# A hybrid attention, retention and expert trunk on one core: probabilities in two steps, the gates made ahead of the first tiles' low parts, rows and 1 / rms made by GpSimd

## The chip, the core and the metric

The kernel runs on one core of a Trainium2 chip. The time is device microseconds of one execution. PE is TensorE, DVE is VectorE, ACT is ScalarE, POOL is GpSimd and SP is SyncE, which here only issues DMAs.

## What is computed

Two layers over 256 rows of 1024 values. Each layer: RMS norm, one input projection of 2304 columns, of which some feed a windowed softmax attention with sinks (8 heads) and the others a gated retention (4 heads); both outputs are concatenated, projected back and added. Then RMS norm and a SwiGLU: dense in layer 0, and in layer 1 eight experts of which each row takes the best two. A last RMS norm ends it. The parts that the change touches are the softmax and the routing:

```
    m = jnp.maximum(jnp.max(s, axis=-1, keepdims=True), sink)
    p = jnp.exp(s - m)
    p = p / (jnp.sum(p, axis=-1, keepdims=True) + jnp.exp(sink - m))
    o = jnp.einsum('bgrcqk,bckgd->bcqgrd', p.astype(v.dtype), vw)
...
    logits = (h @ router_w).astype(f32)
    top_val, top_idx = lax.top_k(logits, TOP_K)
    top_w = jax.nn.softmax(top_val, axis=-1)
    gates = jnp.sum(jax.nn.one_hot(top_idx, N_EXPERTS, dtype=f32) * top_w[..., None], axis=-2)
    y = jnp.zeros_like(h)
    for e in range(N_EXPERTS):
        y = y + gates[..., e:e + 1].astype(h.dtype) * swiglu(h, w_gate[e], w_up[e], w_down[e])
```

## The kernel before

**Weights in pieces.** All weights stream through a ring of 11 slots (`raw`), a unit of 128 x 2048 values each, filled by SP. A unit is worked in two pieces of 128 x 1024. For each piece ACT makes the high part, a rounded copy (`w_hi`, 6 slots, L397 in the front, L417 in the experts), DVE the low part, what is left (`w_lo`, 3 slots, L406 and L424), and PE multiplies in `piece` (L1264): first all products with the high part, activations' high and low tiles (`aT_hi`, `aT_lo`) in turn, then, behind a wait on `lo_vec`, those of the high tiles with the low part. Its last product raises `piece_used`, which frees the slots: DVE may make the low part of piece p once piece p - 3 is used. SP refills a unit's slot when its second low part is made (`lo_vec`).

**The order of work is written out by hand.** On every engine a loop over the pieces s of a mixing stage (26 in a layer: 18 of the input projection, 8 of the output projection) has, at fixed s, the other work in front of the high or low part due there. In DVE's loop (L936) step s makes the low part of piece s + 3 at its end. At s = 7 the scores get bias and maxima, at s = 9 DVE adds up the denominators, takes reciprocals and makes the probabilities in eight operations of 128 x 256 (L979 to L983, chunks 1 and 3 first), each raising `prob_ready`. PE transposes them at s = 12 (`PROB_TURN`, L1365), behind piece 12, when all eight are there. POOL turns the retention's queries and keys (`rope`, L531) at its steps 7 and 9, on two-operand operations between tiles of SBUF.

**The start of the experts.** Behind layer 1's mixing stage PE makes the router's logits; DVE picks the best two of each row (`hot1`, `hot2`), their sum `mask` (L1093), the difference of the two logits (L1095), then 1 / rms (`norm_factor(3)`, L876 to L880) and the scaled gap (L1097) for ACT's exponential `e2` (L775). PE ranks the rows per expert from `mask` (L1494), filling the time with products nobody reads (`keep_busy`). DVE makes `posx` and from it `pick` (L1109), the one-hot matrices with which PE gathers the first pair of experts' rows (`gather`, L1499), high and low parts of the rows (`xg_hi` by ACT, `xg_lo` by DVE, L1151). ACT copies what is gathered into four tiles of `aT_hi` (L782), and `gather_low` (L1111) makes the low tiles on DVE. Tiles 0 and 1 must be there for PE's piece 0, tile 2 for piece 4, tile 3 for piece 6 (L1568).

DVE's order there is: `pick`, the pass count `passes_i` (L1147), `xg_lo`, `gather_low` of tiles 0 and 1 (L1152), the low part of piece 0 (L1154), the slots of the second pass (L1155), then behind ACT's `e2` the gates (L1158 to L1163), the row numbers (L1166, L1167), 1 / rms for every expert (L1168) and a copy (L1169) whose end raises `info_ready`; then it loads the pass count into a register (L1172), enters the loop over passes (L1204) and makes the low parts of pieces 1 and 2 (L1176), and so on. `info` (128 x 2 x 8 x 3: 1 / rms, gate, row) is read by PE in `gather_info` (L1515), behind piece 1 of each even expert, which gives every slot its three numbers; DVE's `slot_info` (L1116) turns them into scales and row addresses. The operations of the gates hang together by semaphores:

```
    def __call__(self, ins):
        self.n += 1
        ins.then_inc(self.sem, 1)
        self.eng.wait_ge(self.sem, self.n)
```

`link(...)` waits for its operation's end, `link.also(...)` only counts it.

POOL's queue (L528) holds at this point: behind `xg_made` the load of the last norm's gain (L582), then the wait for the pass count, its register, and the scatter of each expert's output, which waits for that expert.

Of the kernel before, what the change touches and what calls it, by code (L numbers as in the profile page):

```python
# [11 lines left out]
ALU = mybir.AluOpType  # L12
# [3 lines left out]
P = 128  # L16
SEQ, D_MODEL, DEPTH = 256, 1024, 2
# [63 lines left out]
RET_SCORE = {15: (0, 1), 16: (2, 3)}  # L81
EXP_CHUNKS = {7: (0, 1), 8: (2, 3)}
# [8 lines left out]
C_ALL = C_ROW + TT  # L91
# [8 lines left out]
def constants():  # L100
# [16 lines left out]
    for t in range(TT):  # L117
# [4 lines left out]
        c[:, C_ROW + t] = t * P + n - NO_ROW  # L122
    return c
# [31 lines left out]
def trunk(nc, x, ln_mix, w_in, w_out, rel_bias_table, sinks, ln_ffn, ffn_w_gate, ffn_w_up, ffn_w_down,  # L155
          router_w, exp_w_gate, exp_w_up, exp_w_down, ln_final, consts, buckets, zeros, out):
    with ExitStack() as ctx:
# [49 lines left out]
        def at(name, offset, shape, dt=F32):  # L207

            return nc.alloc_sbuf_tensor_at(name, shape, dt, offset=base_of + offset)
# [36 lines left out]
        passes_f = at("passes_f", 18048, [P, 1])  # L246
        logits_T = at("logits_T", 16384, [N_EXPERTS, SEQ])
# [95 lines left out]
        down_half = sem("down_half")  # L343
        info_ready, row_made, oe_made, scattered = sem("info_ready"), sem("row_made"), sem("oe_made"), sem("scattered")
# [183 lines left out]
        def _(pool):  # L528
# [53 lines left out]
            pool.dma_start(gain_last, ln_final.partition_broadcast(P)).then_inc(gain_landed, 16)  # L582
            pool.wait_ge(route_ready, 1)
# [286 lines left out]
        def _(dve):  # L870
# [46 lines left out]
            for layer in range(DEPTH):  # L917
# [18 lines left out]
                for s in range(MIX_PIECES):  # L936
# [36 lines left out]
                    if s == 9:  # L973
# [5 lines left out]
                        for c0, dst0, src0 in ((1, 0, 0), (1, 64, 64), (0, 0, 64), (0, 64, 0)):  # L979
# [172 lines left out]
            for b in range(2):  # L1152
                gather_low(0, b)
            low_part_e(dve, 0, 0)  # L1154
# [8 lines left out]
            link.also(dve.tensor_tensor(info[:, :, :, 1], gates, tmp, ALU.add))  # L1163
            for t in range(TT):
                step = link if t == TT - 1 else link.also
                step(dve.tensor_scalar(rest[:, t, :], mask[:, t, :], cst[:, C_ROW + t:C_ROW + t + 1], None, ALU.mult))  # L1166
            link.also(dve.scalar_tensor_tensor(out=info[:, :, :, 2], in0=hot2, scalar=float(SEQ), in1=rest, op0=ALU.mult, op1=ALU.add))  # L1167
            link(dve.tensor_copy(info[:, :, :, 0], wide(rstd[:, 2, :])))  # L1168
            dve.tensor_copy(table_first[:], info[:, 0, 0, 0:1]).then_inc(info_ready, 1)  # L1169
# [33 lines left out]

            with dve.Fori(0, n_pass) as r:  # L1204
                with dve.If(r > 0):
                    dve.wait_ge(pick_turned, r)
                    dve.tensor_scalar(info[:, :, :, 2], info[:, :, :, 2], float(ROWS), None, ALU.add).then_inc(info_ready, 1)
# [26 lines left out]
        def _(pe):  # L1234
# [280 lines left out]
            def gather_info(r, e):  # L1515

                pe.wait_ge(info_ready, r + 1)
# [134 lines left out]
```

## Time and profile before

| | us |
|---|---|
| Runs, median of three (lowest, highest) | 1179.99 (1178.19, 1183.70) |
| Profiled execution | 1179.01 |
| Its span | 1177.20 |
| Share of the span that PE, DVE, ACT and POOL are busy | 98%, 81%, 70%, 4% |
| Mean granted clock of PE | 0.996 |

How to read the rows: a time is in us from the span's start. A timeline's row has start, duration, engine, line of the kernel, operation, what it writes and reads with shapes, and the number of operations it merges; a bracket at its end says how long the engine stood idle before it and what ended that. Operations on an engine overlap at their ends, so that starts lie closer together than the durations say. The layer-0 mixing stage runs from about 30 to 104 us, layer 0's dense stage to 292, the layer-1 mixing stage to 385, the router and the start of the experts to about 410, and the experts to the end.

### The profile page before, as it was taken

What the parts mean: (1) busy time and instruction counts of PE and PEld (TensorE: products, weight loads), DVE (VectorE), ACT (ScalarE), POOL (GpSimd) and SP (SyncE); (2) the same over time, 40 slices, a digit from 0 to 9 for tenths busy, and PEclk for the clock granted to TensorE, in tenths of its full rate; (3) what the DMA queues carried; (4) which work ended last, traced back from release to release, by engine and by line L of the source; (5) the groups of instructions that cost most, each with busy time, mean ns of one, the idle gap of its engine ahead of it and who ended that gap; (6) DMA issues with size and microseconds to landing.
All of it is one profiled execution on the core that took longest, in us unless ns stands there. A gap on an engine that the chain in (4) does not pass through costs nothing.

```text
span 1177.2 us, 18157 instructions
## 1 busy us (share of the span) xinstructions
PE 1156.5 (98%) x5954; PEld 971.7 (83%) x5954; DVE 958.5 (81%) x1071; ACT 828.8 (70%) x1003; POOL 43.3 (4%) x57
## 2 busy tenths in 40 slices
PE   9999999999999899999999999999999999999996
PEld 8997888888998688888888888888888888888785
DVE  5867555545676799999899989989999989998996
ACT  6655544433653678788788888878888878888785
POOL 0400000000130000000000000000000000000000
PEclk9999999999999999999999999999999999999999
DMA  9965678556444199999999999999999999999960
GB/s 283 371 190 166 194 248 280 184 179 200 159 154 148 53 348 369 389 385 369 368 337 376 358 398 375 357 345 365 370 394 373 373 339 381 365 369 393 375 271 36
DMA packets 144295, 352.78 MB, mean 300 GB/s; under 512 B 6766, under 2 KB 65342, under 8 KB 144144
## 3 DMA queue, kind: packets, MB, share of 16 engines
q1 hardware_dynamic: 141808, 341.81, 80.3%
q0 software_dynamic: 2032, 9.23, 2.2%
q8 instruction: 50, 0.82, 0.3%
q10 hardware_dynamic: 368, 0.62, 0.2%
q14 instruction: 37, 0.30, 0.1%
HBM read 348.35 MB, written 9.31 MB: 304 GB/s over the span
## 4 chain that ended last, share of the span: by engine, by line
PE 87%; DVE 5%; DMA 3%; ACT 2%; issue 2%; SPq 0%; DVEq 0%; ACTq 0%; POOLq 0%
PE psum L1239 84%; PE psum L1236 3%; DMA raw<-in_w_in 1%; DMA scratch<-oe,row_e 1%; DVE prob L982 1%; DMA back<-scratch 1%; DVE w_lo L424 1%; DVE w_lo L406 1%; DVE smax L966 0%; ACT w_hi L397 0%; DVE score L962 0%; DMA skew<-bias_rows 0%; DVE proj L1015 0%; DVE nmax L967 0%; ACT L723 0%
## 5 line engine op out<-in xcount | busy, mean ns | idle before, releaser
L424 DVE TENSOR_TENSOR w_lo<-raw,w_hi 128x1024 fp32r<-128x1024 f32 x528 | 631.4, 1223 | 47.9 <-PE psum L1239 15.0
L417 ACT ACTIVATE w_hi<-raw 128x1024 fp32r<-128x1024 f32 x528 | 550.6, 1061 | 104.7 <-PE psum L1239 103.6
L1239 PE MATMUL psum<-w_hi,aT_hi 128*128 128x512 f32 (+1 forms) x1232 | 446.1, 371 | 2.6 <-ACT aT_hi L782 1.6
L1239 PE MATMUL psum<-w_hi,aT_lo 128*128 128x512 f32 (+1 forms) x1232 | 439.1, 365 | 0.0
L1239 PE MATMUL psum<-w_lo,aT_hi 128*128 128x512 f32 (+1 forms) x1232 | 323.3, 366 | 5.4 <-DVE w_lo L424 4.6
L1239 PEld LDWEIGHTS psum<-w_hi,aT_hi 128*128 128x128 f32 x1232 | 232.8, 189 | 40.4 <-issue 3.4
L1239 PEld LDWEIGHTS psum<-w_hi,aT_lo 128*128 128x128 f32 x1232 | 232.8, 189 | 35.3
L1239 PEld LDWEIGHTS psum<-w_lo,aT_hi 128*128 128x128 f32 x1232 | 214.4, 189 | 45.0 <-DVE w_lo L424 6.3
L406 DVE TENSOR_TENSOR w_lo<-raw,w_hi 128x1024 fp32r<-128x1024 f32 x118 | 144.8, 1234 | 47.6 <-PE psum L1239 45.8
L397 ACT ACTIVATE w_hi<-raw 128x1024 fp32r<-128x1024 f32 x118 | 124.6, 1060 | 81.0 <-PE psum L1239 74.1
L1239 PE MATMUL psum<-w_hi,heT_hi 128*128 128x512 f32 x352 | 137.8, 391 | 0.0
L1239 PE MATMUL psum<-w_hi,heT_lo 128*128 128x512 f32 x352 | 137.1, 389 | 0.0
L1239 PE MATMUL psum<-w_lo,heT_hi 128*128 128x512 f32 x352 | 108.5, 389 | 0.0
L1239 PEld LDWEIGHTS psum<-w_lo,heT_hi 128*128 128x128 f32 x352 | 66.1, 188 | 13.8
L1239 PEld LDWEIGHTS psum<-w_hi,heT_lo 128*128 128x128 f32 x352 | 66.1, 188 | 13.5
L1239 PEld LDWEIGHTS psum<-w_hi,heT_hi 128*128 128x128 f32 x352 | 66.1, 188 | 13.4
L829 ACT ACTIVATE heT_hi<-psum 128x512 fp32r<-128x512 f32 (+1 forms) x48 | 27.1, 564 | 26.3 <-PE psum L1236 26.3
L1193 DVE TENSOR_TENSOR heT_lo<-psum,heT_hi 128x512 fp32r<-128x512 f32 (+1 forms) x48 | 31.1, 647 | 5.2 <-ACT heT_hi L829 4.8
L824 ACT ACTIVATE hid_e<-psum,info_e 128x512 f32<-128x512 f32 (+1 forms) x48 | 29.5, 651 | 7.3 <-PE psum L1239 7.3
L1239 PE MATMUL psum<-w_hi,hdT_hi 128*128 128x512 f32 x88 | 34.3, 390 | 0.0
L1239 PE MATMUL psum<-w_hi,hdT_lo 128*128 128x512 f32 x88 | 34.3, 389 | 0.0
L1186 DVE SCALAR_TENSOR_TENSOR hid_e<-psum,info_e,hid_e 128x512 f32<-128x512 f32 (+1 forms) x48 | 32.4, 704 | 2.1 <-PE psum L1239 2.1
(194 smaller groups left out, 598.7 us busy)
## 6 DMA issues: line engine op xcount, KB each, us to landing
raw<-in_exp_w_down SPq DMA_DIRECT2D x88, 1024.0 KB, 7.0
raw<-in_exp_w_gate SPq DMA_DIRECT2D x80, 1024.0 KB, 7.0
raw<-in_exp_w_up SPq DMA_DIRECT2D x80, 1024.0 KB, 7.4
raw<-in_w_in SPq DMA_DIRECT2D x17, 1024.0 KB, 5.4
raw<-in_ffn_w_gate SPq DMA_DIRECT2D x22, 512.0 KB, 4.1
raw<-in_ffn_w_up SPq DMA_DIRECT2D x22, 512.0 KB, 5.2
raw<-in_ffn_w_down SPq DMA_DIRECT2D x11, 1024.0 KB, 5.0
raw<-in_w_out SPq DMA_DIRECT2D x8, 1024.0 KB, 8.6
```

The costliest lines, as they stand in the source:

```text
L397: nc.scalar.activation(high_slot(p), raw_piece((p // 2) % RING, p % 2), ACT.Copy).then_inc(hi_made, 1)
L406: eng.tensor_tensor(low_slot(p), raw_piece((p // 2) % RING, p % 2), high_slot(p).bitcast(F32), ALU.subtract).then_inc(lo_vec, 1)
L417: nc.scalar.activation(w_hi[:, q % HIGHS, :], raw_piece(slot, q % 2), ACT.Copy).then_inc(hi_made, 1)
L424: eng.tensor_tensor(w_lo[:, q % LOWS, :], raw_piece(e_slot[q // 2], q % 2), w_hi[:, q % HIGHS, :].bitcast(F32), ALU.subtract).then_inc(lo_ ...
L824: nc.scalar.activation(hid_e[:, c % 2, 0:E_CHUNKS[c][1]], gate_chunk(c), ACT.Silu, scale=info_e[:, e // 2 % 2, j, 0:1]).then_inc(e_gate, 1)
L829: nc.scalar.activation(heT_hi[:, col // P:(col + width) // P, :], psum[:, 4 + c % 2, 0:width].rearrange("p (k t) -> p k t", t=P), ACT.Copy ...
L982: dve.tensor_tensor(prob[:, c, :, dst0:dst0 + 64], score[:, c, :, src0:src0 + 64], r, ALU.mult).then_inc(prob_ready, 1)
L1186: dve.scalar_tensor_tensor(out=part, in0=up_chunk(c), scalar=info_e[:, e // 2 % 2, j, 0:1], in1=part, op0=ALU.mult, op1=ALU.mult).then_inc ...
L1193: dve.tensor_tensor(heT_lo[:, cols, :], psum[:, 4 + c % 2, 0:width].rearrange("p (k t) -> p k t", t=P), heT_hi[:, cols, :].bitcast(F32), A ...
L1236: return pe.matmul(dst, src, ident, is_transpose=True, start=True, stop=True, skip_group_check=True)
L1239: return pe.matmul(dst, a, b, start=start, stop=stop, skip_group_check=True)
```

## The change

Attention's probabilities: four of the eight operations stay at s = 9, the other four move to s = 10, behind the low part of piece 12. At the start of the experts, DVE makes the slots of the second pass and the gates in front of the first `gather_low`, loads its register there too, and leaves the last operation of the gates to raise `info_ready`. The row numbers and the 1 / rms column go to POOL as four operations of 128 x 16 (a product of mask and row, a product of `hot2` and the constant 256, their sum, and ones by 1 / rms), with a semaphore `info_rows` that `gather_info` on PE waits for. The copy L1169 is gone. The constants get one column more.

```diff
+PROB_STEP = {9: ((1, 0, 0), (1, 64, 64)), 10: ((0, 0, 64), (0, 64, 0))}
...
+        row_parts = at("row_parts", 18240, [P, 2, TT, N_EXPERTS])
...
             pool.wait_ge(xg_made, TT)
             pool.dma_start(gain_last, ln_final.partition_broadcast(P)).then_inc(gain_landed, 16)
+            pool.wait_ge(mask_made, 1)
+            mask = mask3[:, 0:TT * N_EXPERTS].rearrange("p (t e) -> p t e", t=TT)
+            row = cst[:, C_ROW:C_ROW + TT].unsqueeze(2).to_broadcast([P, TT, N_EXPERTS])
+            step = cst[:, C_STEP:C_STEP + 1].unsqueeze(2).to_broadcast([P, TT, N_EXPERTS])
+            one = cst[:, C_ONE:C_ONE + TT * N_EXPERTS].rearrange("p (t e) -> p t e", t=TT)
+            pool.tensor_tensor(row_parts[:, 0, :, :], mask, row, ALU.mult).then_inc(row_links, 1)
+            pool.tensor_tensor(row_parts[:, 1, :, :], rt[1][:], step, ALU.mult).then_inc(row_links, 1)
+            pool.wait_ge(row_links, 2)
+            pool.tensor_tensor(info[:, :, :, 2], row_parts[:, 0, :, :], row_parts[:, 1, :, :], ALU.add).then_inc(info_rows, 1)
+            pool.wait_ge(rstd_made, 4)
+            pool.tensor_tensor(info[:, :, :, 0], one, rstd[:, 2, :].unsqueeze(2).to_broadcast([P, TT, N_EXPERTS]), ALU.mult).then_inc(info_rows, 1)
             pool.wait_ge(route_ready, 1)
...
-                        for c0, dst0, src0 in ((1, 0, 0), (1, 64, 64), (0, 0, 64), (0, 64, 0)):
+                    if s in PROB_STEP:
+                        for c0, dst0, src0 in PROB_STEP[s]:
...
-            for b in range(2):
-                gather_low(0, b)
-            low_part_e(dve, 0, 0)
             link.also(dve.tensor_scalar(posx[:, :, 8:16], posx[:, :, 0:8], -float(P), None, ALU.add))
...
-            link.also(dve.tensor_tensor(info[:, :, :, 1], gates, tmp, ALU.add))
-            for t in range(TT):
-                step = link if t == TT - 1 else link.also
-                step(dve.tensor_scalar(rest[:, t, :], mask[:, t, :], cst[:, C_ROW + t:C_ROW + t + 1], None, ALU.mult))
-            link.also(dve.scalar_tensor_tensor(out=info[:, :, :, 2], in0=hot2, scalar=float(SEQ), in1=rest, op0=ALU.mult, op1=ALU.add))
-            link(dve.tensor_copy(info[:, :, :, 0], wide(rstd[:, 2, :])))
-            dve.tensor_copy(table_first[:], info[:, 0, 0, 0:1]).then_inc(info_ready, 1)
+            dve.tensor_tensor(info[:, :, :, 1], gates, tmp, ALU.add).then_inc(info_ready, 1)
 
             dve.wait_ge(route_ready, 1)
             n_pass = dve.value_load(passes_i[0:1, 0:1], min_val=1, max_val=2)
...
+            for b in range(2):
+                gather_low(0, b)
+            low_part_e(dve, 0, 0)
             with dve.Fori(0, n_pass) as r:
                 with dve.If(r > 0):
                     dve.wait_ge(pick_turned, r)
+                    dve.wait_ge(info_rows, 2)
...
                 pe.wait_ge(info_ready, r + 1)
+                pe.wait_ge(info_rows, 2)
```

## Rows read from the trace of the kernel before

**Rows 1.** The page: busy time of the engines, and the last chain by engine.
```profile
PE 1156.5 (98%) x5954; PEld 971.7 (83%) x5954; DVE 958.5 (81%) x1071; ACT 828.8 (70%) x1003; POOL 43.3 (4%) x57
...
PE 87%; DVE 5%; DMA 3%; ACT 2%; issue 2%; SPq 0%; DVEq 0%; ACTq 0%; POOLq 0%
```

**Rows 2.** The waits of PE: who released it, us in total, times, longest.
```profile
PE psum L1239 <- DVE w_lo L424: 4.6, 3, 2.7
PE psum L1239 <- ACT aT_hi L782: 1.6, 1, 1.6
...
PE psum L1239 <- DVE w_lo L406: 0.7, 2, 0.4
```

**Rows 3.** The timeline of PE, layer 0 and 1: start us, us, engine, line, operation.
```profile
55.79 1.22 PE L1239 MATMUL psum<-w_lo,aT_hi 128*128 128x256 f32 x8 [0.37 <-DVE w_lo L406]
...
336.89 1.22 PE L1239 MATMUL psum<-w_lo,aT_hi 128*128 128x256 f32 x8 [0.35 <-DVE w_lo L406]
```

**Rows 4.** The timeline of DVE, layer 1: the probabilities and the rows around them.
```profile
325.09 0.41 DVE L967 SCALAR_TENSOR_TENSOR nmax<-smax,nsinkc 128x4 f32<-128x4 f32 x1
...
326.87 0.16 DVE L967 SCALAR_TENSOR_TENSOR nmax<-smax,nsinkc 128x4 f32<-128x4 f32 x1
...
330.31 5.06 DVE L982 TENSOR_TENSOR prob<-score,rden 128x256 f32<-128x256 f32 x8
335.29 3.00 DVE L406 TENSOR_TENSOR w_lo<-raw,w_hi 128x1024 fp32r<-128x1024 f32 x2
```

**Rows 5.** The timeline of PE at the start of the experts.
```profile
402.67 0.49 PE L1239 MATMUL psum<-w_hi,aT_hi 128*128 128x512 f32 x1 [1.56 <-ACT aT_hi L782]
...
404.85 0.40 PE L1239 MATMUL psum<-w_hi,aT_lo 128*128 128x512 f32 x1
407.94 0.73 PE L1239 MATMUL psum<-w_lo,aT_hi 128*128 128x512 f32 x2 [2.69 <-DVE w_lo L424]
...
409.32 0.49 PE L1239 MATMUL psum<-w_hi,aT_hi 128*128 128x512 f32 x1
...
416.50 0.39 PE L1239 MATMUL psum<-w_hi,aT_hi 128*128 128x512 f32 x1
...
417.86 0.39 PE L1239 MATMUL psum<-w_hi,aT_hi 128*128 128x512 f32 x1
```

**Rows 6.** The timeline of DVE at the start of the experts.
```profile
394.60 0.15 DVE L1095 TENSOR_TENSOR rc<-rc,rc 128x2 f32<-128x2 f32 x1
...
396.02 0.88 DVE L1109 TENSOR_SCALAR pick<-cst,posx 128x128 fp32r<-128x128 f32 x4
...
401.06 1.29 DVE L1113 TENSOR_TENSOR aT_lo<-psum,aT_hi 128x512 fp32r<-128x512 f32 x2 [1.63 <-ACT aT_hi L782]
402.27 1.22 DVE L424 TENSOR_TENSOR w_lo<-raw,w_hi 128x1024 fp32r<-128x1024 f32 x1
...
403.48 0.16 DVE L1158 TENSOR_SCALAR rc<-rc 128x2 f32<-128x2 f32 x1
...
404.37 0.18 DVE L1163 TENSOR_TENSOR info<-rt,rt 128x16 f32<-128x16 f32 x1
...
405.15 0.15 DVE L1169 COPY table_first<-info 128x1 f32<-128x1 f32 x1
406.67 3.50 DVE L424 TENSOR_TENSOR w_lo<-raw,w_hi 128x1024 fp32r<-128x1024 f32 x3 [1.35 <-ACT w_hi L417]
```

**Rows 7.** The register load in DVE's queue, by source line (ns min/median/max).
```profile
L1172 DVEq TENSOR_LOAD <-passes_i x1: 546/546/546, 405.2 to 405.2; - x1
```

**Rows 8.** Stretches of 0.5 us: busy time of the engines, PEclk (granted clock), DMA.
```profile
410.50:411.00 0.50, 0.50 (x3) 0.40 (x2) 0.50 (x2) 0.00 (x0) 0.00 (x0) 0.50 1.07 434
...
413.00:413.50 0.50, 0.50 (x3) 0.40 (x2) 0.50 (x1) 0.00 (x0) 0.00 (x0) 0.50 1.01 418
```

**Rows 9.** The timeline of POOL, layer 1: rope.
```profile
324.15 0.52 POOL L548 TENSOR_TENSOR rope_tmp<-proj,cst 128x128 f32<-128x128 f32 x1
324.75 0.73 POOL L551 TENSOR_TENSOR proj<-proj,rope_tmp 128x256 f32<-128x256 f32 x1
```

More of the change, by code:

```diff
@@ L90 @@
 C_ROW = C_RANK + TT * N_EXPERTS
-C_ALL = C_ROW + TT
+C_STEP = C_ROW + TT
+C_ALL = C_STEP + 1
 CHOSEN = 1000.0
@@ L122, in constants @@
         c[:, C_ROW + t] = t * P + n - NO_ROW
+    c[:, C_STEP] = SEQ
     return c
@@ L343, in trunk @@
         down_half = sem("down_half")
+        info_rows, row_links = sem("info_rows"), sem("row_links")
         info_ready, row_made, oe_made, scattered = sem("info_ready"), sem("row_made"), sem("oe_made"), sem("scattered")
```

## The prediction

> **What bounds the kernel.** I read the busy shares and the last chain first: PE is busy for 98% of the span and makes up 87% of the chain [rows 1]. So a saving on another engine counts only where PE waits for it. The waits of PE are the second view, and they are short: DVE's low parts L424 hold it for 4.6 us in three waits, the longest 2.7, and the low parts L406 for 0.7 us in two [rows 2]. The timelines give the places. The two waits for L406 are one in each layer, 0.37 and 0.35 us, both in front of the low products of a piece of the input projection [rows 3], and in front of both DVE works through eight tiles of probabilities, 5.06 us from 330.31 in layer 1, with the low part next at 335.29 [rows 4]. The wait of 2.69 us is at the first expert: PE starts piece 0 at 402.67, is through with the high products of piece 1 at 405.25 (404.85 and 0.40) and gets that piece's low part at 407.94 [rows 5]. What DVE did meanwhile is in [rows 6]: the low part of piece 0 from 402.27, then the gates, rows and copies from 403.4 to 405.30, a load of a register of 0.55 us from 405.2 [rows 7], the loop's entry, and the low part of piece 1 only at 406.67. Behind this the granted clock is 0.50, that is 1.2 GHz, from 410.50 to 413.50 [rows 8]; PE had been idle for 1.56 and 2.69 us in the eight microseconds before.
>
> **The sum, against the profiled execution's own 1179.01 us** (span 1177.20, 1.81 around it). The median of the three runs is 0.98 above it, and I carry that over at the end.
>
> 1. Probabilities in two steps. DVE does the same eight operations, but the low part of piece 12 now comes after four. By 5.06 / 8 the four end at 330.31 + 2.53 = 332.84, and the low part, 1.5 us beside POOL's rope (3.00 for two), at about 334.3 instead of 336.84. PE asks for it at 336.89 - 0.35 = 336.54, so both waits go: 0.35 + 0.37 = **0.72 us off**. What is late next: the other four end at 334.3 + 2.5 = 336.8, and PE wants them when it has done piece 12's low products, 1.22 behind 336.54, less a little for the last one's tail: 337.6. The next low part ends at 338.3 as before. Margin 0.8 us, so nothing new is waited for. Bounds: 0 if something else holds PE at the same place, 0.72 if not.
>
> 2. Gates first. DVE is idle for 1.63 us before the first `gather_low`, at 399.43 to 401.06 [rows 6]. L1155 and the gates now stand there. L1158 to the start of L1163 took 404.37 - 403.48 = 0.89, so L1163 starts at about 400.3. The register load is issued behind it: in the trace it starts at 405.2, before L1169 has ended, so the queue runs ahead of the engine [rows 6, 7]. From L1169's start at 405.15 the load and its two register operations take until about 406.0, 0.9 us in all; from 400.3 and with the waits of the queue that is 401.35. The first low tile thus starts 0.3 us late, its pair takes 1.29, and PE starts piece 0 at 403.0 instead of 402.67. Hence the low part of piece 0 ends at 403.8 and, with nothing between, that of piece 1 at 403.8 + 3.50 / 3 = 405.0. The loop's entry is now passed by the queue while the 1.22 us low part runs, so I cost it at nothing; without that cover low part 1 would end 0.6 us later and PE wait 0.3 us. PE issues a product each 1.36 / 6 = 0.23 us, so it could have gone on to piece 1's low products at 404.85 + 0.23 = 405.08, and 0.33 later, at 405.41, it can now. The low part is there at 405.0, so they start at 405.41 instead of 407.94: **2.53 us off**, the 0.33 us of lateness being in it.
>
> 3. Rows, 1 / rms and the copy leave DVE: five instructions, 404.46 to 405.30. They are inside the wait of part 2, since everything between the two low parts is; no second saving. Who needs them is PE's gather of the slot data behind piece 1, at about 405.8 now. POOL can begin at the mask, which stands in front of L1095 at 394.60 [rows 6]; even four operations of 0.73 us end at 397.6 or, behind 1 / rms, not much later. Eight microseconds of cover: costed at nothing. POOL's queue holds only the load of the last gain ahead, and nobody waits for what is behind.
>
> 4. The clock. From piece 2's start at 409.32 to piece 7's at 417.86 are 8.54 us for five pieces; at full clock one takes 1.36 (416.50 to 417.86), so 6.80. The half clock costs 1.74 us [rows 5, 8]. With the longer of the two idle stretches gone I expect the clock to hold: **1.74 us off**; bounds 0 and 1.74. DVE keeps up with that: from 405.0 on it has two more pieces by 407.3, a gathered tile (0.65) by 408.0, then a piece, a tile and a piece by 411.0, and PE wants these at 407.7, 409.5 and 411.8.
>
> 5. POOL beside DVE. This goes against the change. In layer 1 DVE's L967 reads two tiles of SBUF and takes 0.16 us with POOL at rest, but 0.41 when it starts at 325.09, and then ends at 325.50, just when POOL's L551 ends (324.75 + 0.73) [rows 4, 9]. So DVE's small two-operand operations wait for the end of POOL's. In the new place POOL's four operations fall on L1095, L877, L878, L880 and L1097, five such ones on the chain to `pick` at 396.02, for which PE waits. POOL's 16 elements aren't in the trace. The nearest rows are 0.52 for 128 and 0.73 for 256 elements [rows 9]; drawn on to 16 that is 0.33. The longest delay is all of POOL's work, 4 x 0.52 = 2.1 us, the least nothing. DVE also has one-operand steps between, and POOL waits for its own links, so I take a third of 4 x 0.33: **0.4 us on**. The Trainium skill, "SBUF — State Buffer", "Who interferes with whom", says that a VectorE operation with two SBUF inputs contends with a GpSimd one that reads SBUF, and whoever comes second is blocked for the whole of the other; the trace agrees by the 0.41. By it alone the price would be up to POOL's whole time.
>
> Sum: 1179.01 - 0.72 - 2.53 - 1.74 + 0.40 = 1174.42; with the 0.98 of the median, **1175.4 us**, 0.4% less. Later stages are bound by PE, and SP's loads start with the low parts, earlier by as much, so the gain goes through to the end.
>
> **Rivals.**
> - The clock falls all the same, since 1.56 us of idle before piece 0 stay and grow by 0.3, and PE is idle for longer before the gather. For it: one fall is all that the trace has here, so which of the two stretches made it can't be told. Against: the fall came behind the longer. 1175.4 + 1.74 = 1177.1.
> - The port. POOL blocks DVE for all of its time, 2.1 instead of 0.4: 1175.4 + 1.7 = 1177.1. For it the ends that meet at 325.50; against, POOL's operations here are 16 elements wide. The page of the Trainium skill named above is the rule behind this one.
> - The split gains nothing, because PE then stands before the transposes of the probabilities: 1175.4 + 0.7 = 1176.1. Its margin of 0.8 us speaks against.
> - The change doesn't do what it says: DVE waits for ACT's exponential before the gates, and that comes late. Then `gather_low` moves behind it; ACT had it well before 399.4 though, as DVE is idle there for the tiles alone. A microsecond late gives 1176.4.
> - Slower: the mark chain of PE is held by POOL for 2.1 us, PE stands idle before the gather, and the clock falls there, so that the gather (32 products, some 4 us from `pick` to the tiles at 401) and the first pieces run at 1.2 GHz. Price 2.1 + 3 for the gather, with the old fall kept (1.74) and another as long (1.74). Against 1175.0, the sum without part 5 and with the median's 0.98, that is 1183.6. It decides from 5.0 us on, where all gains are eaten.
> - More than I see: the three runs lie between 1178.19 and 1183.70, and if the falls of the clock behind this idle stretch make that scatter, the median gains more: some 1173.
>
> **Chances.** My forecast 0.58, the clock 0.14, the port 0.08, the split 0.07, the late exponential 0.03, slower 0.03, more 0.07. The range: at the bottom all gains and no port cost, 1175.0, less the 1.8 us by which the lowest run lies below the median, 1173.2, so 1172.9 with the last case touched; at the top the clock and half of the port's extra together, 1175.4 + 1.74 + 0.85 = 1178.0, so 1178.2. What a measurement of this kernel can tell from no change is about 0.5%, 5.9 us. My own case gains 4.6, so faster by more than that takes the last case or a favourable scatter in mine: 0.18. Slower by as much needs more than the worst case: 0.01. Within: 0.81.
>
> **What would show it.** Right: no wait of PE for L406 in either layer; PE's low products of piece 1 follow its high ones with no idle; first low tile at about 0.3 us behind ACT's; clock 1.00 from 396 to 420; L1095 to `pick` 0.2 to 0.6 us longer than the 1.42 us of before. Wrong: a clock of 0.50 anywhere behind the gather; a new wait of PE for POOL's rows, or for `prob`; DVE idle between the low parts of pieces 0 and 1; low parts from piece 3 on that PE waits for.

## The result, and the profile after

| | before | after |
|---|---|---|
| Median of six runs, us (lowest, highest) | 1180.95 (1178.19, 1183.70) | 1174.15 (1172.70, 1174.66) |
| Profiled execution, us | 1179.01 | 1173.32 |
| Its span, us | 1177.2 | 1171.5 |
| Mean granted clock | 0.996 | 0.998 |

The ratio is 0.9941, with a 95% interval of 0.9925 to 0.9956: the kernel is 0.6% faster, by 4.4 to 7.5 thousandths. The line numbers below are those of the kernel after: `piece` multiplies at L1252, DVE's low parts are L412 and L430, `gather_low` is L1131, the last of the gates L1178.

The waits of PE (total us, times, longest) answer to [rows 2]:

```profile
PE psum L1252 <- ACT w_hi L403: 1.7, 1, 1.7
PE psum L1252 <- DVE aT_lo L1131: 1.7, 1, 1.7
PE psum L1252 <- DVE w_lo L430: 1.6, 2, 1.3
```

The 2.69 us behind L430 and both waits for the low parts of the front (0.35 and 0.37) are gone. What is left at L430 are two waits in the last experts, 1.31 us (1.61 before) and 0.34 us as before. The wait before piece 0 (1.68 us) is as long as it was, and DVE's low tile ends it, where ACT's high tile did. The 1.7 us for ACT's L403 is at the kernel's start and belongs to no part of the change: the kernel before has it too in its two later profiles (e11 and e12 below).

The probabilities in layer 1, on DVE (to [rows 4]) and the piece behind them on PE (to [rows 3]):

```profile
329.86 1.98 DVE L1000 TENSOR_TENSOR prob<-score,rden 128x256 f32<-128x256 f32 x4
331.76 1.55 DVE L412 TENSOR_TENSOR w_lo<-raw,w_hi 128x1024 fp32r<-128x1024 f32 x1
333.23 3.17 DVE L1000 TENSOR_TENSOR prob<-score,rden 128x256 f32<-128x256 f32 x4
```

```profile
335.93 1.12 PE L1252 MATMUL psum<-w_lo,aT_hi 128*128 128x256 f32 x8
336.89 1.91 PE L1249 MATMUL psum<-cst,prob 128*128 128x128 f32 x16
```

The low part of piece 12 now ends at 333.31; PE asks for it at 335.93, goes on without a pause, and turns the probabilities from 336.89, half a microsecond after the last of them (333.23 + 3.17 = 336.40).

The start of the experts, DVE (to [rows 6]), then PE (to [rows 5]):

```profile
393.54 0.15 DVE L1113 TENSOR_TENSOR rc<-rc,rc 128x2 f32<-128x2 f32 x1
...
395.01 0.87 DVE L1127 TENSOR_SCALAR pick<-cst,posx 128x128 fp32r<-128x128 f32 x4
...
399.30 0.18 DVE L1178 TENSOR_TENSOR info<-rt,rt 128x16 f32<-128x16 f32 x1
400.24 1.29 DVE L1131 TENSOR_TENSOR aT_lo<-psum,aT_hi 128x512 fp32r<-128x512 f32 x2 [0.76 <-ACT aT_hi L799]
401.45 4.62 DVE L430 TENSOR_TENSOR w_lo<-raw,w_hi 128x1024 fp32r<-128x1024 f32 x4
```

```profile
401.78 0.49 PE L1252 MATMUL psum<-w_hi,aT_hi 128*128 128x512 f32 x1 [1.68 <-DVE aT_lo L1131]
...
403.97 0.40 PE L1252 MATMUL psum<-w_hi,aT_lo 128*128 128x512 f32 x1
404.20 0.62 PE L1252 MATMUL psum<-w_lo,aT_hi 128*128 128x512 f32 x2
...
405.47 0.49 PE L1252 MATMUL psum<-w_hi,aT_hi 128*128 128x512 f32 x1
...
412.41 0.39 PE L1252 MATMUL psum<-w_hi,aT_hi 128*128 128x512 f32 x1
```

Four low parts follow each other from 401.45, where 3.2 us lay between the first and the second. Piece 1's low products start 0.23 us behind its last high one. From piece 2 (405.47) to piece 7 (412.41) are 6.94 us instead of 8.54. The clock, in stretches with the columns of [rows 8] (the third number from the right is the granted clock; 1.00 is 2.4 GHz):

```profile
402.00:406.00 4.00, 4.00 (x22) 3.32 (x22) 4.00 (x5) 4.00 (x5) 0.00 (x0) 1.00 0.21 32
406.00:410.00 4.00, 4.00 (x19) 3.27 (x18) 3.97 (x9) 2.44 (x4) 0.00 (x0) 1.00 1.00 396
```

This profile is at half clock only at its very end, from 1166.9 us, where PE has no products left. Every profile here ends so, the one of before from 1171.5, and the mean clock of the table counts this stretch too.

POOL's four new operations, in its timeline:

```profile
393.71 0.21 POOL L594 TENSOR_TENSOR row_parts<-mask,cst 128x16 f32<-128x16 f32 x1 [2.94 <-DVE mask L1111]
393.89 0.21 POOL L595 TENSOR_TENSOR row_parts<-rt,cst 128x16 f32<-128x16 f32 x1
394.18 0.23 POOL L597 TENSOR_TENSOR info<-row_parts 128x16 f32<-128x16 f32 x1
394.70 0.22 POOL L599 TENSOR_TENSOR info<-cst,rstd 128x16 f32<-128x16 f32 x1 [0.30 <-DVE rstd L897]
```

They take 0.21 to 0.23 us and are over at 394.92, almost ten microseconds before PE asks for the rows. DVE's chain from L1113 to `pick` is 395.01 - 393.54 = 1.47 us beside them; it was 396.02 - 394.60 = 1.42.

So the profiles alone, by the same product of PE in both: at piece 12's low part of layer 1 the new kernel is 0.96 us ahead (336.89, 335.93), at the experts' first product 0.89 (402.67, 401.78), at piece 1's low part 3.74 (407.94, 404.20), at piece 7 5.45 (417.86, 412.41), at the end 5.7. The forecast's sum was 4.59. Of the 0.96 us at the first of these, 0.72 are the two waits, the rest lies further up and belongs to no part of the change; of the last step, from 5.45 to 5.7, 0.3 us are the shorter wait at the last experts. The medians are further apart, by 6.8 us: the kernel before has a median 1.94 us above its profiled execution, the kernel after one 0.83 above. The experiments had to explain that gap as well.

### The profile page after: what moved, and what is told of

Read it like the earlier page. It is cut to its first block, busy times and chain, and to the rows that moved or that the text cites. A ratio compares the mean times of both kernels' runs of the same rounds, so it can differ in the third digit from the quotient of the medians.

```text
span 1171.5 us, 18160 instructions
## 1 busy us (share of the span) xinstructions
PE 1152.5 (98%) x5954; PEld 969.0 (83%) x5954; DVE 957.4 (82%) x1066; ACT 828.5 (71%) x1003; POOL 44.6 (4%) x61
## 4 chain that ended last, share of the span: by engine, by line
PE 92%; DVE 2%; DMA 2%; ACT 2%; issue 1%; DVEq 0%; SPq 0%; ACTq 0%; POOLq 0%
PE psum L1252 89%; PE psum L1249 3%; DMA scratch<-oe,row_e 1%; DMA raw<-in_w_in 1%; DMA back<-scratch 1%; DVE w_lo L430 0%; ACT w_hi L403 0%; DVE proj L1033 0%; ACT L740 0%; DVE w_lo L412 0%; ACT proj L740 0%; ACT aT_hi L726 0%; DVE x_sb L926 0%; ACT o_sq L734 0%; DVE proj L1040 0%
## 5 line engine op out<-in xcount | busy, mean ns | idle before, releaser
L430 DVE TENSOR_TENSOR w_lo<-raw,w_hi 128x1024 fp32r<-128x1024 f32 x528 | 630.8, 1221 | 45.3 <-PE psum L1252 13.8
L1252 PE MATMUL psum<-w_hi,aT_hi 128*128 128x512 f32 (+1 forms) x1232 | 445.6, 371 | 4.0 <-ACT w_hi L403 1.7
L1252 PE MATMUL psum<-w_hi,aT_lo 128*128 128x512 f32 (+1 forms) x1232 | 438.6, 365 | 0.0
L1252 PE MATMUL psum<-w_lo,aT_hi 128*128 128x512 f32 (+1 forms) x1232 | 322.2, 365 | 1.6 <-DVE w_lo L430 1.6
L1252 PEld LDWEIGHTS psum<-w_hi,aT_hi 128*128 128x128 f32 x1232 | 232.3, 189 | 41.6 <-issue 3.5
L1252 PEld LDWEIGHTS psum<-w_hi,aT_lo 128*128 128x128 f32 x1232 | 232.5, 189 | 35.1
L1252 PEld LDWEIGHTS psum<-w_lo,aT_hi 128*128 128x128 f32 x1232 | 214.0, 189 | 40.5 <-DVE w_lo L430 3.1
L412 DVE TENSOR_TENSOR w_lo<-raw,w_hi 128x1024 fp32r<-128x1024 f32 x118 | 144.9, 1234 | 47.7 <-PE psum L1252 45.9
L403 ACT ACTIVATE w_hi<-raw 128x1024 fp32r<-128x1024 f32 x118 | 124.5, 1059 | 81.4 <-PE psum L1252 74.2
L1252 PE MATMUL psum<-w_hi,heT_hi 128*128 128x512 f32 x352 | 137.8, 391 | 0.0
L1252 PE MATMUL psum<-w_hi,heT_lo 128*128 128x512 f32 x352 | 137.1, 389 | 0.0
L1252 PE MATMUL psum<-w_lo,heT_hi 128*128 128x512 f32 x352 | 108.5, 389 | 0.0
L1252 PEld LDWEIGHTS psum<-w_lo,heT_hi 128*128 128x128 f32 x352 | 66.1, 188 | 13.8
L1252 PEld LDWEIGHTS psum<-w_hi,heT_lo 128*128 128x128 f32 x352 | 66.1, 188 | 13.5
L1252 PEld LDWEIGHTS psum<-w_hi,heT_hi 128*128 128x128 f32 x352 | 66.1, 188 | 13.4
L611 POOL DMA_INDIRECT scratch<-oe,row_e x7 | 9.3, 1332 | 663.8 <-ACT oe L810 560.6
L1252 PE MATMUL psum<-w_hi,hdT_hi 128*128 128x512 f32 x88 | 34.3, 390 | 0.0
L1252 PE MATMUL psum<-w_hi,hdT_lo 128*128 128x512 f32 x88 | 34.3, 389 | 0.0
```

Source lines behind the costliest of these rows:

```text
L403: nc.scalar.activation(high_slot(p), raw_piece((p // 2) % RING, p % 2), ACT.Copy).then_inc(hi_made, 1)
L412: eng.tensor_tensor(low_slot(p), raw_piece((p // 2) % RING, p % 2), high_slot(p).bitcast(F32), ALU.subtract).then_inc(lo_vec, 1)
L430: eng.tensor_tensor(w_lo[:, q % LOWS, :], raw_piece(e_slot[q // 2], q % 2), w_hi[:, q % HIGHS, :].bitcast(F32), ALU.subtract).then_inc(lo_ ...
L611: pool.indirect_dma_start(scratch, bass.IndirectOffsetOnAxis(ap=row_e[:, v % 2, j:j + 1], axis=0), oe[:], None, bounds_check=2 * ROWS - 1, ...
L1252: return pe.matmul(dst, a, b, start=start, stop=stop, skip_group_check=True)
```

## The experiments

Two theories stood at the beginning. By the first (A), the three savings add up as forecast, and the half clock follows PE's idle of 2.69 us. By the second (B), the clock falls for the idle before piece 0, or for any, and its recovery has nothing to do with the moved gates. There is one profile of each kernel, and three of the kernel before. Savings "by the ratio" are the ratio to the kernel before, run beside it, times its 1180 us; an interval in brackets is the 95% interval of the ratio.

### The split alone, and all but the split

```diff
 e1_split: the kernel before, and
+PROB_STEP = {9: ((1, 0, 0), (1, 64, 64)), 10: ((0, 0, 64), (0, 64, 0))}
...
-                        for c0, dst0, src0 in ((1, 0, 0), (1, 64, 64), (0, 0, 64), (0, 64, 0)):
+                    if s in PROB_STEP:
+                        for c0, dst0, src0 in PROB_STEP[s]:
 e2_no_split: the kernel after, and
-PROB_STEP = {9: ((1, 0, 0), (1, 64, 64)), 10: ((0, 0, 64), (0, 64, 0))}
+PROB_STEP = {9: ((1, 0, 0), (1, 64, 64), (0, 0, 64), (0, 64, 0))}
```

> The kernel before with the probabilities in two steps alone. By my sum both waits of PE for the low part of piece 12 go and nothing else moves: 0.7 us off (0.72), idle 2.69 us and the half clock at the first expert as before. By the rival that PE then stands before the transposes: 0, and a wait of PE for prob shows. A third, that the split also moves the start of the experts against the clock's fall, would give 0.7 and up to 1.7 more.

> The changed kernel with all eight probabilities in one step again. By my sum it keeps all but 0.7 to 0.9 us of the gain: some 5 us off the kernel before by the spans, idle in front of piece 1's low products gone, clock at 1.00. If the split had part in keeping the clock up, the half clock is back: 3.3 us off.

The split alone: 1178.78 us median, ratio 0.9989 (0.9977 to 1.0001), 1.3 us by the ratio. All but the split: 1175.29, ratio 0.9960 (0.9948 to 0.9973), 4.7 us by the ratio, where the whole change had 0.9941. The interval of the split reaches from 2.7 us to just beyond nothing, so the runs alone don't show it; that of the rest reaches from 3.2 to 6.1 us. In the traces the wait for the low part of piece 12 is absent in the one (PE waits for L426 three times, all at the experts) and back with 0.7 us in two in the other. The half clock at the first expert is still there with the split alone, and its profile shows something new in the windows:

```profile
407.00:408.00 1.00, 0.75 (x2) 0.65 (x3) 1.00 (x2) 0.00 (x0) 0.00 (x0) 0.50 0.00 0
...
412.00:413.00 1.00, 1.00 (x4) 0.71 (x4) 0.15 (x1) 0.22 (x1) 0.00 (x0) 0.50 1.01 381
...
414.00:415.00 1.00, 1.00 (x6) 0.83 (x5) 0.68 (x5) 0.37 (x1) 0.00 (x0) 1.00 0.30 119
```

The clock is at half from 406.8 to 413.6, for 6.8 us and not for 3.4, though PE's wait is the same (2.76 us, from 404.5 to 407.25). It falls within that wait, 2.3 us after its start; in the profile of before it fell 2.4 us after the wait's end (410.36, 407.94).

### The move without POOL

```diff
 e3_move_only: the kernel before, without the copy L1169 (the copy of 1 / rms raises info_ready), and
-            for b in range(2):
-                gather_low(0, b)
-            low_part_e(dve, 0, 0)
...
+            for b in range(2):
+                gather_low(0, b)
+            low_part_e(dve, 0, 0)
             with dve.Fori(0, n_pass) as r:
```

> The kernel before, with the first two low tiles and the low part of piece 0 moved behind gates and rows, all made by DVE, nothing on POOL (the copy L1169 is left out). DVE then comes to the first low tile some 0.75 us later than in the changed kernel, 0.95 us behind ACT's high tile, so PE stands idle for 2.4 instead of 1.7 us before piece 0 and then never for 2 us. Theory A (the clock falls for the idle in front of piece 1's low products): clock stays 1.00, 4.0 us off before. Theory B (any idle of over 2 us there): clock 0.50 for 3.4 us, 2.4 us off.

1176.86 us, ratio 0.9974 (0.9963 to 0.9985), 3.1 us, between the 4.0 of theory A and the 2.4 of theory B. The timeline of PE and the windows:

```profile
403.75 0.49 PE L1238 MATMUL psum<-w_hi,aT_hi 128*128 128x512 f32 x1 [2.37 <-ACT w_hi L417]
...
407.64 0.71 PE L1238 MATMUL psum<-w_lo,aT_hi 128*128 128x512 f32 x2
```

```profile
404.00:405.00 1.00, 1.00 (x4) 0.76 (x4) 1.00 (x2) 1.00 (x2) 0.00 (x0) 0.70 0.00 0
...
406.00:407.00 1.00, 1.00 (x4) 0.80 (x3) 1.00 (x2) 0.83 (x1) 0.00 (x0) 0.50 0.17 20
...
408.00:409.00 1.00, 1.00 (x11) 0.95 (x9) 1.00 (x3) 0.61 (x1) 0.00 (x0) 1.00 1.00 401
```

Now there is no wait in front of piece 1's low products, PE is idle for 2.37 us before piece 0, and the clock is at half from 404.4 to 407.8. Theory A in its narrow form is wrong: it isn't that one place. The idle before piece 0 can bring the fall as well when it is longer than the 1.49 to 1.68 us that it lasts in the kernels before and after. It need not: two of the twelve executions had a mean clock of 0.997 and 0.998, like the kernel after, and took 1174.99 and 1174.66 us. That makes POOL's part worth something that I had costed at nothing: with rows and 1 / rms on DVE, the first low tile comes later (at 402.22, 0.9 us behind ACT's tile, where the kernel after is 0.2 behind), and the clock goes with it. Run side by side, the means of this kernel and of e2, which differ in POOL's part alone, are 1.7 us apart.

### POOL without the move

```diff
 e4_pool_only: the kernel after, the probabilities in one step, and
+            for b in range(2):
+                gather_low(0, b)
+            low_part_e(dve, 0, 0)
             link.also(dve.tensor_scalar(posx[:, :, 8:16], posx[:, :, 0:8], -float(P), None, ALU.add))
...
-            for b in range(2):
-                gather_low(0, b)
-            low_part_e(dve, 0, 0)
             with dve.Fori(0, n_pass) as r:
```

> Rows and 1 / rms on POOL and the copy gone, but the two low tiles and the low part of piece 0 in front of the gates as before, no split. DVE's work between the two low parts is shorter by 0.8 us, so PE's idle is 1.9 instead of 2.69. Theory A with the fall bound to the length of this idle: if 1.9 us is short enough, clock stays at 1.00 and 0.8 + 1.7 = 2.5 us off; if not, 0.8 us off. POOL's price on the chain to pick shows too: 0.05 us as in the changed kernel.

1179.34 us, ratio 0.9993 (0.9982 to 1.0003): no difference that these runs can tell, 0.8 us by the ratio. PE's wait is shorter by 0.7 us, as expected, and the clock falls:

```profile
407.24 1.00 PE L1252 MATMUL psum<-w_lo,aT_hi 128*128 128x512 f32 x2 [1.98 <-DVE w_lo L430]
```

```profile
408.00:409.00 1.00, 1.00 (x7) 0.96 (x5) 1.00 (x2) 0.72 (x1) 0.00 (x0) 0.50 0.73 86
```

Of this profile 6.8 us (from 407.5) are at half clock. So 1.98 us of idle, 1.49 before piece 0 ahead of it, were still too much in this execution; shortening the wait without ending it brought about its own length, and that within the error.

### The idle filled, with DVE no faster

In both kernels PE makes products in unused banks that nobody reads, 11 in the long idle or 6 in the short one.

```diff
 e5_fill_long: the kernel before, and in piece(), between its high and its low products (between is 11 for piece 1 of the first expert, else 0)
+                for again in range(between):
+                    mm(bank(6 + again % 2), w_hi[:, 1, 0:P], w_hi[:, 1, 0:512], True, True)
 e6_fill_short: the kernel before, and
             gather(4)
+            pe.wait_ge(hi_made, FRONT_PIECES + 1)
+            fill(6)
```

> The kernel before, and PE makes 11 products that nobody reads (128x512, 0.23 us each, 2.5 us) between the high and the low products of the first expert's piece 1, in the idle of 2.69 us. DVE's low part comes no earlier. Theory A (that idle makes the clock fall): clock stays at 1.00 and the 1.6 to 1.7 us of the half clock alone are saved. Theory B (the 1.56 us before piece 0 make it fall, or it falls at any rate): clock 0.50 for 3.4 us as before, no gain.

> The kernel before, and PE makes 6 products that nobody reads (1.4 us) behind the gather, in the idle of 1.56 us in front of piece 0; the idle of 2.69 us stays. Theory A: clock falls as before, no gain. Theory B: clock stays at 1.00 and 1.7 us are saved. If both idle stretches are needed for the fall, both this and the other fill keep it up.

The long one filled: 1177.11 us, ratio 0.9978 (0.9969 to 0.9987), 2.6 us. The short one filled: 1180.00, ratio 1.0000 (0.9989 to 1.0011). PE and a window of the clock, in the first and in the second:

```profile
405.25 2.67 PE L1239 MATMUL psum<-w_hi 128*128 128x512 f32 x11
408.15 0.74 PE L1239 MATMUL psum<-w_lo,aT_hi 128*128 128x512 f32 x2 [0.24 <-DVE w_lo L424]
...
411.00:412.00 1.00, 1.00 (x6) 0.84 (x5) 1.00 (x1) 0.81 (x1) 0.00 (x0) 1.00 1.01 418
```

```profile
401.08 1.55 PE L1239 MATMUL psum<-w_hi 128*128 128x512 f32 x6
...
408.07 0.72 PE L1239 MATMUL psum<-w_lo,aT_hi 128*128 128x512 f32 x2 [2.75 <-DVE w_lo L424]
...
411.00:412.00 1.00, 1.00 (x4) 0.81 (x3) 1.00 (x2) 0.47 (x1) 0.00 (x0) 0.50 1.01 418
```

In the first, piece 1's low products come at 408.15 (407.94 before), DVE has done nothing sooner, and the clock stays at 1.00 to the end of the experts. This is the clock's term by itself: 2.6 us, by the interval 1.5 to 3.7, where 1.6 to 1.7 were expected. In the second the 1.55 us before piece 0 are full, the 2.75 us stay, and the clock is at half from 410.5 for 3.4 us, as before. Between these two the case is decided: in the kernel before it is the wait for piece 1's low part that brings the clock down.

### Why the clock's term is larger than in the profile

```
 e11_before_again, e12_before_third: the kernel before, unchanged
```

> The kernel before once more, for its clock. If the half clock at the first expert lasts longer in some executions than in the one profiled first, a profile like those of the split alone and of POOL alone (0.50 for 6.8 us, mean clock 0.995, 3.4 us lost) shows here too, and its span is 1.7 us longer than 1177.2. If those two kernels had it by their own edits, it is 3.4 us again.

> The kernel before a third time, for a profile of an execution whose mean clock is 0.995, as in 52 of its 75 executions so far. By my reading that profile has 0.50 for 6.8 us at the first expert where those of mean clock 0.996 have 3.4, and the pieces 2 to 7 take 10.2 us instead of 8.54. If the lower mean comes from the end of the kernel, where PE has nothing to do, the stretch at the expert is 3.4 us again. If this execution is one of 0.996 the question stays with the profiles of the split alone and of POOL alone.

The first of the two had a mean clock of 0.996 and 3.4 us at half (span 1176.7), like the profile that the prediction was made from. The second had 0.995 (span 1179.5). Its windows, and PE (the last row is piece 7's start):

```profile
409.00:410.00 1.00, 0.79 (x2) 0.70 (x3) 1.00 (x2) 0.00 (x0) 0.00 (x0) 0.61 0.00 0
...
412.00:413.00 1.00, 1.00 (x3) 0.81 (x4) 1.00 (x2) 0.00 (x0) 0.00 (x0) 0.50 1.00 414
...
416.00:417.00 1.00, 1.00 (x5) 0.85 (x5) 0.48 (x5) 0.21 (x1) 0.00 (x0) 0.98 0.20 78
```

```profile
409.21 1.22 PE L1239 MATMUL psum<-w_lo,aT_hi 128*128 128x512 f32 x2 [2.74 <-DVE w_lo L424]
...
420.67 0.39 PE L1239 MATMUL psum<-w_hi,aT_hi 128*128 128x512 f32 x1
```

The same kernel, the same wait (2.74 us), and 6.8 us at half. From piece 1's low products to piece 7 are 420.67 - 409.21 = 11.46 us; in the first profile 417.86 - 407.94 = 9.92, in the kernel after 412.41 - 404.20 = 8.21. The fall thus costs 1.7 us in one kind of execution and 3.25 in the other. The pieces 2 to 7 alone take 8.89 us (411.78 to 420.67), where 10.2 were expected: here the fall comes with piece 1's low products, at 409.2, and 1.3 us of it are paid before piece 2.

Over the 94 executions of the kernel before that stand beside these experiments, 63 had a mean clock of 0.995 or less and took 1180.5 us on average, 31 had 0.996 or more and took 1178.3. (The expectation above counts 52 of 75; up to there they were 55 of 78.) None of the 12 executions with the long idle filled and none of the 6 of the kernel after had 0.995 or less, so most of the 63 should have the longer stretch at the experts. That is argued and not shown, because the mean doesn't say where the clock was at half. The profile of e6 has a mean of 0.995 with 3.4 us at the experts; its other 3.4 us are at the kernel's start, behind idle of 0.94 and 1.69 us (PE, then a window):

```profile
8.13 1.09 PE L1236 MATMUL psum<-cst,x_sb 128*128 128x128 f32 x8 [0.94 <-DMA x_sb<-in_x]
10.91 0.40 PE L1239 MATMUL psum<-w_hi,aT_hi 128*128 128x256 f32 x1 [1.69 <-ACT w_hi L397]
...
12.00:13.00 1.00, 1.00 (x6) 1.00 (x6) 1.00 (x4) 1.00 (x2) 0.00 (x0) 0.50 1.10 349
```

And the two averages are 2.1 us apart, where the two kinds of fall differ by 1.54. What is shown is that the profile that the prediction was made from had the shorter stretch, and that the longer exists.

### POOL's share of the port

```diff
 e7_pool_more: the kernel after, POOL's first two products six times over
+            for again in range(6):
+                pool.tensor_tensor(row_parts[:, 0, :, :], mask, row, ALU.mult).then_inc(row_links, 1)
+                pool.tensor_tensor(row_parts[:, 1, :, :], rt[1][:], step, ALU.mult).then_inc(row_links, 1)
+                pool.wait_ge(row_links, 2 * again + 2)
 e9_pool_wide: the kernel after, and in front of POOL's rows
+            for again in range(4):
+                pool.tensor_tensor(bias[:, 0:2, :], bias[:, 2:4, :], bias[:, 2:4, :], ALU.mult).then_inc(row_links, 1)
+                pool.wait_ge(row_links, again + 1)
```

> The changed kernel with POOL's first two products made six times over: 12 operations of 0.2 us instead of 2, some 2.9 us of POOL's work from the mask on, over the whole of DVE's chain to pick and its start of xg_lo. By the port's rule (a two-operand operation of DVE waits for the end of POOL's) the chain from L1113 to pick is 0.3 to 0.6 us longer than 1.47 us, and so is the kernel. By the reading that operations this small hardly meet: under 0.1 us.

> The changed kernel with four products of 128x256 on data that nobody needs (0.73 us each alone) on POOL, from the mask on, in front of its rows; its rows come 3 us later and are still in time. By the port's rule with a hold as long as the operation runs, DVE's two-operand operations L1113, L894, L895, L897 and L1115 each wait for the end of one of POOL's, as L984 did beside rope: the chain from L1113 to pick grows from 1.47 us to 2.5 to 3.5, PE's gather and the end come 1 to 2 us later. If small operations slip in between, as beside the twelve of 16 elements, the chain stays at 1.47.

Twelve operations of 16 elements: 1173.38 us, ratio 0.9945 (0.9930 to 0.9960), no slower than the kernel after, and the chain is 394.92 - 393.46 = 1.46 us. In the last two products it is POOL that gives way: beside DVE's low parts of the rows they take 1.15 and 1.19 us instead of 0.21, while those low parts take 2.37 us (2.36 in the kernel after).

```profile
393.63 0.21 POOL L595 TENSOR_TENSOR row_parts<-mask,cst 128x16 f32<-128x16 f32 x1 [2.93 <-DVE mask L1112]
...
396.12 1.15 POOL L595 TENSOR_TENSOR row_parts<-mask,cst 128x16 f32<-128x16 f32 x1
```

Four operations of 256 elements: 1174.15 us, ratio 0.9958 (0.9943 to 0.9973), span 1172.3 where the kernel after had 1171.5. DVE's chain, then POOL:

```profile
393.72 0.53 DVE L897 TENSOR_TENSOR newton<-rstd 128x2 f32<-128x2 f32 x1
394.28 0.16 DVE L898 TENSOR_TENSOR newton<-newton,rstd 128x2 f32<-128x2 f32 x1
394.48 0.47 DVE L899 TENSOR_SCALAR newton<-newton 128x2 f32<-128x2 f32 x1
...
395.18 0.46 DVE L1118 TENSOR_TENSOR rc<-rc,rstd 128x2 f32<-128x2 f32 x1
...
395.83 1.15 DVE L1130 TENSOR_SCALAR pick<-cst,posx 128x128 fp32r<-128x128 f32 x4
```

```profile
393.62 2.69 POOL L595 TENSOR_TENSOR bias<-bias 128x256 f32<-128x256 f32 x4 [2.94 <-DVE mask L1114]
```

Three of DVE's operations are stretched to about half a microsecond, and the ones behind them slip in at 0.16. `pick` starts at 395.83, 2.38 us behind the chain's start (393.45): 0.9 us more than the 1.47 of the kernel after, a little below the 2.5 that was the least expected. It is stretched too (1.15 us instead of 0.87 for its four operations), so that PE's gather starts 1.2 us later against the chain's start (3.68 us behind it, at 397.13, where the kernel after has 2.50). L899 and `pick` have a single tensor operand; the expectation had named only two-operand ones, so that part of my reading is wrong or not the whole. PE stood idle for 1.39 us before the gather and 1.70 before piece 0, and the clock stayed at 1.00.

### Two steps further

```diff
 e8_tile_by_tile: the kernel after, the register load in front of the slots and gates, and in piece()
+                    if first_tile is not None:
+                        pe.wait_ge(g_hi, first_tile + n)
+                        pe.wait_ge(g_lo, first_tile + n)
 e10_low_first: that, and behind the register load
+            low_part_e(dve, 0, 0)
+            for b in range(2):
+                gather_low(0, b)
+            low_part_e(dve, 0, 1)
             link.also(dve.tensor_scalar(posx[:, :, 8:16], posx[:, :, 0:8], -float(P), None, ALU.add))
```

> The changed kernel, with DVE's register load moved in front of the slots and gates (right behind the low parts of the rows, which run for 2.4 us), and piece 0 of a pair of experts waiting for tile 0 before its first bank and tile 1 before its second, instead of for both. DVE is then at the first low tile when ACT's high tile is there, 0.2 us earlier, and PE starts one tile (0.6 us) earlier with half of piece 0's high products. Both together: PE's idle before piece 0 from 1.68 to about 0.9 us, of which up to 0.6 us comes off the time (0.2 and 0.46 less what is waited for again inside the piece). If the idle is only shifted into piece 0: 0.2 us.

> The version with tile by tile and early register load, and DVE's order now: low parts of the rows, register, low part of piece 0, the two low tiles, low part of piece 1, and only then slots and gates. The low part of piece 0 (1.15 us) falls mostly into DVE's idle of 0.56 us before the first low tile, so that tile is up to 0.5 us later, but the low part of piece 1 ends 0.7 to 1.1 us earlier. PE starts its first products at 0.8 to 1.2 us behind the gather, waits no more for L430 in piece 0, and comes to piece 2 some 0.3 to 0.8 us earlier than in the version without. The gates end 1.1 us behind that, about when PE asks for the slot data: if they are late, 0.3 us of this is given back. Total: 1172.5 to 1173.0. No half clock.

The first: 1173.33 us, ratio 0.9943 (0.9928 to 0.9959). PE starts 0.79 us behind the gather, and then waits for the low part inside piece 0:

```profile
401.00 0.47 PE L1252 MATMUL psum<-w_hi,aT_hi 128*128 128x512 f32 x1 [0.79 <-DVE aT_lo L1131]
...
402.64 0.73 PE L1252 MATMUL psum<-w_lo,aT_hi 128*128 128x512 f32 x2 [0.34 <-DVE w_lo L430]
...
405.40 0.47 PE L1252 MATMUL psum<-w_hi,aT_hi 128*128 128x512 f32 x1
```

From the gather's start to piece 2 it takes 405.40 - 396.15 = 9.25 us; the kernel after, 405.47 - 396.04 = 9.43. The idle was moved into the piece, and 0.2 us were gained. The second: 1172.96 us, ratio 0.9945 (0.9932 to 0.9957), the lowest median of all. Piece 2 starts 404.49 - 395.87 = 8.62 us behind the gather's start, 0.8 us better than in the kernel after, of which 0.4 are lost again at pieces 5 and 6, where DVE, now late with the gates, is just behind. Both medians are below that of the change (1174.15), but the intervals overlap almost wholly, and the profiled spans are 1171.6 and 1171.1 us where the kernel after has 1171.5. The traces show 0.2 and 0.4 us gained at this place; that either kernel is faster as a whole is not shown.

## Why the prediction came out as it did

The time, 1174.15 us, lies in the range (1172.9 to 1178.2), 1.25 us below the forecast of 1175.4. The chances were less good: the ratio's 0.6% is past the bound of 0.5% by a little, where I had given 0.81 to staying within it and 0.18 to this. Its interval holds both.

1. **Probabilities in two steps, 0.72 us off.** Right. Both waits went, PE came to the transposes half a microsecond behind the last probability, where I had 0.8 of margin, and the medians with and without the split are 1.1 to 1.5 us apart, with an error as large.
2. **Gates first, 2.53 us off.** Right in mechanism and nearly in size. The wait of 2.69 us was gone; from the first expert product to piece 1's low part it takes 2.42 us instead of 5.27, so 2.85 off, less the 0.07 by which PE fell behind on the way from piece 12 to the first product. I had charged 0.33 us for the late low tile; DVE was only 0.2 behind: the low tile began 0.94 us behind the start of the last gate (399.30, 400.24), where I had counted 1.05 for the register load (400.3, 401.35). The loop's entry cost nothing, as assumed: the low parts follow at once.
3. **Rows on POOL, nothing.** For the rows themselves this held, with almost ten microseconds to spare. But it was wrong by omission to call them no second saving because they lay inside the wait of part 2. With the move they would have stood in front of the first low tile: e3 shows PE idle for 2.37 us there and the clock at half behind it. The parts don't add up one by one; the move is worth less without POOL.
4. **The clock, 1.74 us off.** Right that it holds, and right about which idle it was (e5, e6). This is the term that was mis-sized. It was 1.6 us between the two profiles (8.54 to 6.94), but my upper bound of 1.74 is no bound: an execution of the kernel before lost 3.25 us at this place (e12), and filled by itself the idle gave 2.6 (e5). I had taken one profile's 3.4 us for the kernel's. Of the distance between my 4.6 us and the 6.8 of the medians 0.9 is this. A small slip beside it: PE's idle of 1.56 us began at 401.1, nine and not eight microseconds before the fall. I had written that a scatter by the clock would make the median gain more, but only as the last rival, at 0.07.
5. **POOL beside DVE, 0.4 us on.** Much too high: 0.05 us. It went by the line through 0.52 and 0.73 us to 0.33 for 16 elements; they take 0.21, and of DVE's small operations beside them only L896 is longer, 0.23 us instead of 0.17. L894, with two operands, takes its usual 0.16 from 393.81 on, though by the rows POOL is at work from 393.71 to 394.10; POOL's times are rough. The rule of the Trainium skill ("SBUF — State Buffer", "Who interferes with whom") shows where POOL's operations are wide: in e9 L897, from 393.72, ends at 394.25, about when the first of POOL's four (393.62, 2.69 / 4 each) does. By it alone I would have erred further.

With terms of 0.7, 2.8, 2.6 and 0.05 the sum is 6.05 us, inside the measured 5.2 to 8.9. The remaining 0.75 is within the error of the medians and has no name.

The rivals: the clock did not fall all the same, but the fear was near the truth, as 2.0 us (e4) and 2.4 us (e3) of idle still brought it down in the profiles. The port cost 0.05 us at this width. "More than I see", with the scatter made by the falls of the clock, was right in its mechanism, though not in full: the measured time is 1.2 us above its 1173. The split did not end before the transposes. ACT's exponential was there in time. The slower case needed 2.1 us of POOL on the way to `pick` and a fall of the clock in the gather: e9 put 1.39 us of idle in front of the gather and no fall came there or behind it.

## What to carry to other kernels

A wait of the matmul engine at the end of a dense stretch has two prices, its own length and what the clock takes behind it; here the second (2.6 us) was as large as the first, and it could be measured by itself by filling the wait with products that nobody reads. Before sizing such a term, take more than one profile: one shows one of the kinds. The mean clock of further executions tells that there are others, but not where in the kernel they differ. And when small work is moved in front of a hand-over, add up all that now stands there: the same move was worth 3.1 us with the rows in it and 4.7 us with them on the idle engine, by ratios whose intervals overlap (1.8 to 4.4, 3.2 to 6.1).

## What the runs showed of the hardware

- The half clock (1.2 GHz) came in portions: 3.4 us in some executions and 6.8 in others of the same kernel with the same wait (2.69 and 2.74 us).
- At the start of the experts it came with idle stretches of PE of 1.98, 2.37 and 2.69 to 2.76 us, and not with 1.39 and 1.70, with 1.68, or with 1.49 and 0.24. It fell between 0.5 us before the end of the wait (e1) and 2.4 us behind it (before and e6). One profile of each kernel stands behind this but for the kernel before, which has three. At the kernel's start one profile (e6) had 3.4 us at half behind 0.94 and 1.69 us of idle, where e5, with 1.70 us before the same product, had none.
- POOL's product of two tiles of 128x16 took 0.21 us, and 1.15 to 1.19 beside DVE's 128x1024 subtraction of two tiles in SBUF. Four POOL products of 128x256 stretched three of DVE's operations on two columns from 0.16 or 0.17 to 0.46 to 0.53 us, one with a single tensor operand among them.
- A register load in DVE's queue took 0.55 us, with 0.22 us of register operations behind it. Where it ran beside the low parts of the rows (e8, from 396.3) and not behind the gates, DVE began the low tile 0.2 us sooner against the gather (DVE's idle 0.56 instead of 0.76 us).
